# State updates in pairs on row groups, squares summed on column groups, first tiles of out and up interleaved, drains ahead of weight parts

## The reference

```python
xn = rmsnorm(x, norm1_g)
z = xn @ w_in + b_in                       # 1024 -> 4368, split into the inputs of four branches
log_a = log_sigmoid(a_lr @ w_alpha2 + b_alpha) / 16
o_gla, gla_new = gla_recurrence(q, k, v, log_a, s0)      # chunks of 64 tokens:
#   att = tril(q_in @ (k*exp(-bcum)).T); o = att @ v + q_in @ s; s = exp(b_last)*s + (k*exp(b_last-bcum)).T @ v
o_a = rmsnorm(o_gla, gla_norm_g) * silu(a_r)             # over the 128 values of each of 4 heads
o_b = gelu(b_u) * gmlp_spatial(layernorm(gelu(b_v)))
o_c = silu(layernorm(causal_depthwise_conv(c_a * sigmoid(c_g), width 31)))
o_d = sliding-window attention with sinks (prompt, and sample against a cache)
x = x + (sum_i sigmoid(xn @ w_gate + b_gate)_i * (o_i @ w_branch[i])) @ w_out
g, up = split(rmsnorm(x, norm2_g) @ w_gate_up);  x = x + (silu(g) * up) @ w_down
```

## Time and profile before

| | us |
|---|---|
| median of 3 runs | 1132.93 |
| lowest, highest | 1130.41, 1137.48 |
| the profiled execution | 1131.63 |
| its span, first to last instruction | 1129.8 |

### The profile page before, as it was taken

How to read it: one execution, slowest core, us unless ns; L and a number is a source line. 1 busy time by engine, 2 the same in 40 slices (tenths; PEclk the granted TensorE clock), 3 DMA queues, 4 the chain that set the end, 5 groups by cost and what they waited for, 6 DMA issues and landing times.

```text
span 1129.8 us, 20168 instructions
## 1 busy us (share of the span) xinstructions
PE 1095.0 (97%) x8400; PEld 1067.2 (94%) x8400; DVE 707.3 (63%) x1014; ACT 598.2 (53%) x892; POOL 459.7 (41%) x250
## 2 busy tenths in 40 slices
PE   5999999999999999999999998999999999999999
PEld 5899988999999999999999997989999999999998
DVE  7695879451786655565548967883438755655543
ACT  5554664777545544444446557547673554444432
POOL 2578734676363111110166766537645521111000
PEclk9999999999999999999999999999999999999999
DMA  7745442344446576556545454334444655455652
GB/s 244 223 151 201 131 132 94 131 149 141 160 149 221 163 216 194 169 163 181 166 147 166 148 171 166 96 110 131 150 148 143 192 177 180 154 171 156 187 161 92
DMA packets 61483, 181.42 MB, mean 161 GB/s; under 512 B 16048, under 2 KB 18736, under 8 KB 60720
## 3 DMA queue, kind: packets, MB, share of 16 engines
q1 hardware_dynamic: 60816, 176.37, 49.0%
q10 hardware_dynamic: 576, 3.76, 0.9%
HBM read 174.87 MB, written 7.27 MB: 161 GB/s over the span
## 4 chain that ended last, share of the span: by engine, by line
PE 89%; DVE 4%; ACT 4%; issue 1%; DMA 1%; SPq 0%; ACTq 0%; DVEq 0%
PE ps L416 28%; PE ps L418 27%; PE ps L417 27%; ACT w_hi L783 1%; DVE zg_r L1139 1%; ACT work L871 1%; DVE w_lo L1134 1%; DMA raw<-in_w_z 1%; DVE qz L1329 1%; DVE x_lo L1481 0%; PE ps L451 0%; PE ps L428 0%; PE ps L675 0%; DVE work L1460 0%; DVE zg L1504 0%
## 5 line engine op out<-in xcount | busy, mean ns | idle before, releaser
L416 PE MATMUL ps<-x_hi,w_hi 128*128 128x288 f32 x1952 | 584.4, 299 | 18.9 <-DVE x_lo L1149 10.8
L417 PE MATMUL ps<-x_lo,w_hi 128*128 128x288 f32 x1952 | 576.6, 295 | 0.0
L418 PE MATMUL ps<-x_hi,w_lo 128*128 128x288 f32 x1952 | 574.8, 294 | 0.0
L783 ACT ACTIVATE w_hi<-raw 128x1024 fp32r<-128x1024 f32 x316 | 328.8, 1054 | 311.6 <-PE ps L418 294.7
L1572 POOL TENSOR_TENSOR w_lo<-raw,w_hi 128x1024 fp32r<-128x1024 f32 x131 | 338.4, 2594 | 204.0 <-ACT w_hi L783 203.9
L416 PEld LDWEIGHTS ps<-x_hi,w_hi 128*128 128x128 f32 x1952 | 366.7, 188 | 25.7 <-issue 12.0
L418 PEld LDWEIGHTS ps<-x_hi,w_lo 128*128 128x128 f32 x1952 | 368.4, 189 | 0.0
L417 PEld LDWEIGHTS ps<-x_lo,w_hi 128*128 128x128 f32 x1952 | 367.4, 188 | 0.7
L1134 DVE TENSOR_TENSOR w_lo<-raw,w_hi 128x1024 fp32r<-128x1024 f32 x185 | 232.0, 1255 | 138.2 <-ACT w_hi L783 138.2
L1596 POOL TENSOR_TENSOR work<-work,rs 128x288 f32<-128x288 f32 x44 | 35.8, 814 | 239.5 <-ACT work L1096 239.5
L418 PE MATMUL ps<-h_hi,w_lo 128*128 128x288 f32 x352 | 104.4, 296 | 0.0
(11 more groups left out here) (230 smaller groups left out, 1026.1 us busy)
## 6 DMA issues: line engine op xcount, KB each, us to landing
raw<-in_w_up SPq DMA_DIRECT2D x88, 512.0 KB, 3.9
raw<-in_w_z SPq DMA_DIRECT2D x68, 512.0 KB, 3.5
raw<-in_w_gate SPq DMA_DIRECT2D x64, 512.0 KB, 3.4
raw<-in_w_branch SPq DMA_DIRECT2D x32, 512.0 KB, 3.4
raw<-in_w_down SPq DMA_DIRECT2D x32, 512.0 KB, 3.6
raw<-in_w_out SPq DMA_DIRECT2D x16, 512.0 KB, 3.4
raw<-in_w_down SPq DMA_DIRECT2D x16, 384.0 KB, 3.2
kv<-in_state ACTq DMA_DIRECT2D x2, 1024.0 KB, 5.9
```

The costliest lines, as they stand in the source:

```text
L416: pe.matmul(out, wh, rh, start=start, stop=False)
L417: pe.matmul(out, wh, rl, start=False, stop=False)
L418: return pe.matmul(out, wl, rh, start=False, stop=stop)
L783: act.activation(w_hi[:, slot, :], raw[:, slot, :], ACT.Copy).then_inc(hi_done, 1)
```

## The change

It does six things.

1. ACT drains the tile of the block before ahead of the w_hi of a later block, in z from tile 9 on and in the gates.
2. The scores are issued in the order of their four 64 x 64 quadrants, the four small ones behind them all.
3. The updates of chunks 0 and 1 are issued together, and those of 2 and 3, with the two row halves by turns; the products with the state move to slots 41, 42 and 43, and smp_old thereby to slot 43.
4. The sums of squares go to one group of 32 partitions per head in one bank; ACT makes the power of 288 columns; a new step in slot 50 spreads the four row groups to all partitions with four matmuls of a constant, from which DVE multiplies in two instructions out of PSUM.
5. In out, the first four units of tile 0 are followed by the w_hi matmuls of the first four units of tiles 1 and 2. In up, the first six units of tiles 0 and 1 come ahead of the last two of both; the sum of squares comes after U1.
6. At the end of the branches DVE makes w_lo behind the merged parts of the same block, in out behind the drain and the normed part. ACT and DVE make the parts of U2 and U3 ahead of n2_rstd.

```diff
@@ tensor, split_mm becomes hi_mm (L416, L417) followed by lo_mm (L418)
@@ tensor, att_in
-                for par in range(2):
-                    r = slice(64 * par, 64 * par + 64)
-                    for hp in range(2):
-                        for ch in range(NSEG):
...
+                for hp in range(2):
+                    for ch in range(0, NSEG, 2):
+                        for par in range(2):
+                            r = slice(64 * par, 64 * par + 64)
+                            for odd in range(2):
...
+                                pe.matmul(ps[64 * odd:64 * odd + 64, 4 + par, col:col + 64], k_neg[r, hp, tok],
+                                          qz[r, 2 * hp + par, tok], start=True, stop=True)
@@ tensor, chunks
+                def updates(a):
+
                     for k in range(2):
-                        mm = pe.matmul(ps[:, 4 + ch % 2, k * 256:k * 256 + 256], k_tok[rows, a, k * P:(k + 1) * P],
-                                       v_tok[rows, a, k * 256:k * 256 + 256], start=True, stop=True)
+                        for odd in range(2):
+                            rows = slice(64 * odd, 64 * odd + 64)
+                            mm = pe.matmul(ps[:, 4 + odd, k * 256:k * 256 + 256], k_tok[rows, a, k * P:(k + 1) * P],
+                                           v_tok[rows, a, k * 256:k * 256 + 256], start=True, stop=True)
                     mm.then_inc(E("update"), 1)
...
+                updates(0)
+                yield from at("chunk1")
+                from_state(1)
+                yield from at("chunk2")
+                pe.wait_ge(E("state_step"), l * NSEG + 2)
+                updates(1)
+                from_state(2)
+                yield from at("chunk3")
+                from_state(3)
@@ tensor, gla_sums and the new step
                 for h in range(4):
-                    mm = pe.matmul(ps[:, (2, 3, 6, 7)[h], 0:T], c("ones"), z[:, A_V + h, :], start=True, stop=True)
+                    mm = pe.matmul(ps[TS * h:TS * h + TS, 2, 0:T], c("ones", TS), z[:, A_V + h, :], start=True, stop=True)
...
+                yield from at("gla_spread")
+                pe.wait_ge(E("gla_rstd"), l1)
+                for h in range(4):
+                    r = slice(TS * h, TS * h + TS)
+                    mm = pe.matmul(ps[:, GLA_BANKS[h], 0:T], c("spread")[r], gla_rs[r], start=True, stop=True)
+                mm.then_inc(E("gla_spread"), 1)
@@ tensor, out
+                early = KC - 4
...
+                for u in range(early):
+                    out_part(0, u)
+                for t in (1, 2):
+                    bank_wait(pe, l, TO + t)
+                    pe.wait_ge(hi_done, g0 + O0 + t + 1)
+                    for u in range(early):
+                        hi_mm(ps[:, t, 0:T], (g0 + O0 + t) % RING, u, m_hi[:, u, :], m_lo[:, u, :], u == 0)
+                for u in range(early, KC):
+                    mm = out_part(0, u)
...
@@ tensor, up
+                late = KC - 2
+                for t, parts in [(0, range(late)), (1, range(late)), (0, range(late, KC)), (1, range(late, KC))] \
+                        + [(t, range(KC)) for t in range(2, 2 * HC)]:
...
-                    if t == 0:
+                    if t == 1 and parts[-1] == KC - 1:
 
                         pe.wait_ge(squares, (2 * l + 1) * (KC - 1))
                         sum_of(7, sq[:, 0, :], "n2_sums")
@@ scalar, gla_rstd
-                for h in range(2):
-                    act.activation(g_tmp[:, 2 * h:2 * h + 2, :], ps[:, 2 + 4 * h:4 + 4 * h, 0:T], ACT.Ln, scale=1.0 / P,
-                                   bias=c("eps6", 1))
+                act.activation(gla_rs, ps[:, 2, 0:T], ACT.Ln, scale=1.0 / P, bias=c("eps6", 1))
@@ scalar, loops over z and gates
                 for t in range(NZ):
+                    if t > C_TILES:
+                        drain_z(l, t - 1)
                     split(g0 + t + 3)
...
                 for t in range(4 * KC):
-                    split(g0 + G0 + t + 3)
                     if t == 0:
                         drain_z(l, NZ - 1)
                     else:
                         drain_gate(l, t - 1)
+                    split(g0 + G0 + t + 3)
@@ scalar, ahead of n2_rstd
+                split(g0 + U0 + 2)
+                split(g0 + U0 + 3)
                 logs()
@@ vector, state steps
-                    dve.wait_ge(E("update"), l * NSEG + ch + 1)
+                    dve.wait_ge(E("update"), l * 2 + ch // 2 + 1)
@@ vector, a_out
-                dve.wait_ge(E("gla_rstd"), l1)
-                link(dve.scalar_tensor_tensor(out=g_tmp, in0=gla_o, scalar=p("gla_g"), in1=g_tmp, op0=ALU.mult, op1=ALU.mult), l)
+                dve.wait_ge(E("gla_spread"), l1)
+                for h in range(0, 4, 2):
+                    ins = dve.scalar_tensor_tensor(out=g_tmp[:, h:h + 2, :], in0=gla_o[:, h:h + 2, :], scalar=p("gla_g"),
+                                                   in1=ps[:, GLA_BANKS[h]:GLA_BANKS[h] + 2, 0:T], op0=ALU.mult, op1=ALU.mult)
@@ vector, branches and out
-                    split(g0 + BR0 + b + 3)
+                    if b <= 12:
+                        split(g0 + BR0 + b + 3)
...
                         for k in (2 * (b - 13), 2 * (b - 13) + 1):
                             merged_part(l, k)
+                        if b != 2 * KC - 2:
+                            split(g0 + BR0 + 16 if b == 13 else g0 + BR0 + 17)
                 for k in (KC - 2, KC - 1):
                     merged_part(l, k)
+                split(g0 + BR0 + 18)
```

More of the change, by code:

```diff
@@ L592, in mixers @@
                     mm.then_inc(E("update"), 1)
-                    if ch >= 1:
-                        pe.wait_ge(E("state_step"), l * NSEG + ch)
-                        for k in range(2):
-                            out = ps[:, 2 + a, :].rearrange("p (h i) -> p h i", h=4)
-                            mm = pe.matmul(out[:, 2 * k:2 * k + 2, 64 * (ch % 2):64 * (ch % 2) + 64], state[:, k, :],
-                                           qz[:, 2 * k:2 * k + 2, ch * 64:ch * 64 + 64], start=False, stop=True,
-                                           skip_group_check=True)
-                        mm.then_inc(E("chunk_out"), 1)
@@ L602, in mixers, with from_state @@
-                    if ch == 1:
-                        yield
+                def from_state(ch):
+                    pe.wait_ge(E("state_step"), l * NSEG + ch)
+                    out = ps[:, 2 + ch // 2, :].rearrange("p (h i) -> p h i", h=4)
+                    for k in range(2):
+                        mm = pe.matmul(out[:, 2 * k:2 * k + 2, 64 * (ch % 2):64 * (ch % 2) + 64], state[:, k, :],
+                                       qz[:, 2 * k:2 * k + 2, ch * 64:ch * 64 + 64], start=False, stop=True,
+                                       skip_group_check=True)
+                    mm.then_inc(E("chunk_out"), 1)
```

80 lines of the change are left out of this document (52 added, 28 removed).

## The result

Runs taken side by side: the kernel before 1131.67 us (median of 4, 1129.13 to 1137.48), the changed kernel **1118.45 us** (median of 4, 1115.78 to 1120.38). The ratio is 0.9886, 95% interval 0.986 to 0.9911: 1.14% less, so on the far side of the 1% that a measurement can tell from no change, with the interval reaching across it. The forecast was 1120.8, its range 1115 to 1127. The profiled execution has a span of 1115.1 us against 1129.8.

The account below looks back on a forecast made before the run. PE was taken as the bound, busy 97% of 1129.8 us, so only its stalls and small matmul groups could gain. Terms gave 6.06 us a layer, 12.1 for two: 1119.5 from 1131.6, 1120.8 on the median; range 1115 to 1127.

Parts of the forecast that it names:

- drain behind tile 15: After z tile 15, ACT drains before making w_hi, so PE starts at 73.82: 0.94 us gained a layer.
- drain behind tile 32: After tile 32, PE starts earlier but POOL's w_lo holds DVE's scaling of probabilities: 0.38 us gained, bounds 0.38 and 0.95.
- gMLP chain: Chain at L1238 begins just behind a POOL piece that now comes later: loses between 0 and 0.38 us, taken as 0.16.
- scores and their drain: Quadrant scores need 1.5 us or less, the drain ends last at 170.28, PE goes at 170.43: 0.56 us gained.
- state updates: Chunk slots: paired updates remove two state waits, 8.95 us becomes 5.93 plus a new 0.93 wait behind smp_old: 2.09 gained.
- cv_mean: DVE's convolution ends about 1.4 us later and L428 waits for it: costs between 0 and 1.0 us, taken as 0.05.
- squares without cv_mean: Sums of squares on column groups take 0.71 us and the spread 0.88, against 1.94: 0.35 us gained a layer.
- up: First tiles of up: no stall there, U5's w_lo done at 377.55 just ahead of 377.64: 0 gained, bound 0.6 lost.
- A: The gain is handed to the next wait, at cv_mean, U5 and out: 3.5 us a layer, 1125.9 us; chance 0.25.
- B: Contention of POOL and DVE is milder, 1.11 us a layer stay: 1118.6, or 1116.7 with L610's wait hidden; chance 0.08.
- C: Column and row groups do not overlap; sums and spread cost 1.94 each, 2.5 us more a layer: 1125.8; chance 0.08.
- D: Slower: weights become late, 57 ACT-drained blocks a layer cost 0.38 each, 43 us in all: 1164 us; chance 0.05.

Follow-up runs that it names:

- both drain runs: ACT's drains put back behind the weight parts in the changed kernel, 1125.24 us; drains put first, and nothing else, in the kernel before, 1126.42 us.
- drain order undone: Changed kernel with ACT's drains behind the weight parts again, as before the change: 1125.24 us.
- score order undone: Changed kernel with the score matmuls in their old order, head pair by head pair with the sample's scores between them: 1119.17 us.
- updates undone: Changed kernel with PE's eight state updates one after the other, each followed by its product from the state, as before: 1120.91 us.
- more taps: Changed kernel with ACT's copy of smp_old in slot 44 and DVE's convolution tap runs 3 and 4 steps long instead of 1 and 3: 1113.76 us.
- squares undone: Changed kernel with the sums of squares as four full matmuls into four banks and no spread matmuls, as before: 1117.39 us.
- plain order in out: Changed kernel with PE's tiles of out one after the other again, up left interleaved: 1120.18 us.
- plain order in up: Changed kernel with PE's tiles of up one after the other again, out left as changed: 1116.64 us.
- the later copy: Changed kernel with ACT's copy of smp_old moved from behind the gelu of slot 42 to slot 44: 1115.67 us.
- drain order alone: Kernel before with ACT's drains put ahead of the weight parts and nothing else: 1126.42 us.

## Why the prediction held, step by step

| step, us a layer | forecast | measured | by |
|---|---|---|---|
| drain behind tile 15 | 0.94 | 0.95 | both drain runs |
| tile 15 itself | 0 | 0.29 | both drain runs |
| drain behind tile 32 | 0.38 | 0.47 | trace |
| gMLP chain | -0.16 | 0.05 | trace |
| scores and their drain | 0.56 | 0.62 | drain order, score order undone |
| state updates | 2.09 | 2.34 | updates undone |
| cv_mean | -0.05 | -0.14 | updates undone, more taps |
| squares without cv_mean | 0.35 | 0.22 | squares undone |
| first tiles of out | 1.95 | 1.94 | plain order in out |
| up | 0 | -0.05 | trace; plain order in up |
| sum | 6.06 | 6.69 | |

**The drains.** The 0.94 behind tile 15 came true to 0.01. The bound chosen for tile 32 was the right one: POOL was first (132.72 against 133.13), DVE's scaling ended at 133.13 + 4.16 = 137.29, and measured from the end of PE's block that is 2.31 where it was 139.61 - 138.63 = 0.98: later by 1.33, the 0.95 and 0.38 of the forecast. PE gained 0.47, not 0.38, since by then ACT's copies of the first transposes were done. What the prediction missed is 0.29 at tile 15: there ACT squares q and k (L845 before, L903 after) from drained tiles, and with the drain ahead of the split the squares are ready before PE asks. In the trace before, PE began the sums of these squares 0.20 late, at 67.66 with its last block's last matmul at 67.33 and a pace of 0.133, and paid some 0.10 to restart; after, they begin without a gap. The step that failed is the list of stalls itself: it was read from the list of waits, which counts idle time from the end of a matmul's record. That record is 0.29 long where the next one could start after 0.133, so this stall shows there as 0.04. The loss for the gMLP chain did not come; its wait is 0.6 in both kernels.

**The scores.** 0.56 was forecast with scores of 1.5 or less; they took 0.94. That changed nothing, since the drain ended last, as the forecast had it.

**The updates.** The small groups summed to 5.93 + 0.93; they took 6.66 in all. The new wait behind smp_old, 0.11 + 0.19 + 0.48 + 0.15 = 0.93, is in the trace: with the forecast's 1.90 for it, L634 (from 189.01) is through at 190.91, 0.11 ahead of ACT's copy, and 191.84 - 190.91 = 0.93. Mis-sized was the product ahead of smp_old, 0.54 in place of 0.64 (188.47 to 189.01), and the edges by the rest. The term for cv_mean was the one without a row, between 0 and 1.0; 0.14 is near its low end.

**The squares.** The sums' 0.71 and the spread's 0.88 (measured 0.89) hold; left out was the 0.10 that the full matmul behind the narrow ones pays. The Trainium skill, TensorEngine Tiling, section Tiling Modes, says that a change of mode drains TensorE; the trace agrees and gives a size: about 0.10 to enter (L654 starts at 210.04, 0.23 behind the matmul ahead of it and not 0.133) and 0.10 to leave, so a group in another form has two edges.

**Up.** Nothing gained, as forecast, and 0.05 lost at the place that the forecast named. The low weight part of U5 (L1194, from 368.18) is done at 369.40, and PE's first matmul of U5 starts at 369.50, its second 0.20 behind it in place of 0.133. The forecast had 377.55 against 377.64 for the same pair, and a loss of 0.6 as its bound.

**The rivals.** A (handed on) hardly happened in the change: cv_mean took 0.14 and U5 0.05. Both were also named as signs of a wrong forecast; both came, too small for the list of waits. But it is just what the later copy ran into, 0.85 of 0.90. B (milder contention, 1118.6) met the total of 1118.4 and had the wrong reason: contention was as forecast, the surplus came from tile 15 and the updates. C fell: four narrow sums took 0.71 us, not 1.94. (Its price was summed wrongly: 2 x 1.94 - 0.71 - 0.88 is 2.3 a layer and not 2.5.) D fell: no wait for a weight part stands in any list here, also with the splits of slots 31, 37 and 64 each put back further; U5's 0.05 is all that the blocks show.

**The total.** 13.3 us inside the layers against 12.1 forecast, 1.2 us of the 2.4 between 1120.8 and 1118.4; the rest is within what the start does to a median of four.

## What to carry to other kernels

On an engine that serves both a pipeline's banks and its prefetch, put what someone waits for now ahead of what someone waits for three blocks later: this was worth 1.7 us a layer by itself and 3.4 in the changed kernel, and it has a price: GpSimd's pieces behind the later split start later and hold VectorE (behind tile 32 PE gained 0.47 us of 0.95). A wait removed has a successor; before moving work, look for the next thing that is late and for idle time on that engine to pay it from (0.9 us a layer came only after 0.85 of taps had been moved into DVE's idle time). Value parts of a change by undoing each as well as by doing each alone (two edits at the scores gave 0.62 together and nothing without each other), and read small steps from blocks of the trace, not from medians.

## What the hardware showed beyond expectation

**Who starts first holds the other.** For operations with two inputs in SBUF, DVE and GpSimd took turns by whole instructions: whichever began second ran on only when the first was through (the same scaling took 4.16 us begun second and 2.29 begun first, GpSimd's piece 3.60 begun second and 2.40 otherwise). The Trainium skill, GPSIMD Engine Reference, section 1 Specifications, says that GpSimd shares its SBUF interfaces with VectorE and contends with its instructions of two SBUF inputs; the traces agree, and in them the order of the starts decides who pays. In the start of the first layer this tips by about a tenth of a microsecond. The timelines of DVE and POOL, first with the drain order undone, then with the drain order alone:

```profile
40.91 5.62 DVE L1545 SCALAR_TENSOR_TENSOR x_lo<-work,prm,x_hi 128x288 fp32r<-128x288 f32 x8
43.58 2.63 POOL L1644 TENSOR_TENSOR w_lo<-raw,w_hi 128x1024 fp32r<-128x1024 f32 x1 [3.68 <-ACT w_hi L841]
```

```profile
40.56 3.52 DVE L1481 SCALAR_TENSOR_TENSOR x_lo<-work,prm,x_hi 128x288 fp32r<-128x288 f32 x8
43.63 2.69 POOL L1572 TENSOR_TENSOR w_lo<-raw,w_hi 128x1024 fp32r<-128x1024 f32 x1 [4.08 <-ACT w_hi L783]
```

Eight steps, 0.43 us apart: begun at 40.56, the last starts 0.06 ahead of POOL's piece and gets through; begun 0.35 later, it starts 0.34 behind the piece and is held, and PE stands still 1.9 us for it. The profile of the kernel before has this stall, that of the changed kernel has not. DVE's beginning follows an earlier POOL piece, which follows a load's landing; nothing in the change touches these. Among fourteen profiles three have the stall: before, drain order undone, score order undone. In these three the last step starts 0.13 to 0.45 behind POOL's piece, in the other eleven 0.02 to 0.26 ahead of it. It is 2.5 us of the difference of the spans, and not the change's.

**The clock in the start.** Against that, the changed kernel's profile lost 1.5 us. Its windows of 5 us (us, PE busy, granted clock, DMA share, GB/s), then those of the run with more taps:

```profile
20.00:25.00 5.00, 4.12 (x18) 0.66 0.00 0
```

```profile
20.00:25.00 5.00, 4.00 (x28) 1.00 0.00 0
```

A mean of 0.66 of the 2.4 GHz: from 21.9 to 24.6 us the matmuls stood 0.24 us apart in place of 0.133, the 1.2 GHz level. Ahead of it PE had stood idle 1.98 us, waiting for the sum of the squares (L438 for L1524). Six of the fourteen profiles have this drop. The length of that wait doesn't decide it: with the score order undone it was 2.3 us and the clock stayed at 1.00 there. That profile lost its clock later: from 48.0 to 51.4 us the granted clock was 0.50 and the matmuls stood 0.24 apart, behind the stall of 1.9 us told above; the other two profiles with that stall kept 1.00. What decides it stays open. All of this lies in the first 52 us, ahead of where the inner time begins, and it is large enough to explain why the medians 1115.7, 1117.1, 1117.4 and 1118.4 of kernels whose inner times lie within 0.5 us do not rank them.
